# Weight chunks loaded in halves and split in quarters, with one TensorE wait per quarter

## What is computed

```python
h = jnp.pad(x @ w_in, ((0, 0), (PAD, 0), (0, 0)))
ya = window_gqa(qa, ka, va, sink) * jax.nn.silu(ga)        # A: banded attention, 4 heads
ob = diff_attention(qb, kb, vb, lam, valid)                # B: dense differential attention, 4 heads
y_f = hgrn2_chunked(qc, k_f, ic, logf_f)                   # C: gated linear recurrence, both directions
y = jnp.concatenate([ya, yb, yc], axis=-1)[:, PAD:]
return y @ w_out
...
h = layer_norm(ALPHA * h + y, ln_g[l], ln_b[l])
```

## Time and profile before

| | |
|---|---|
| median of 3 runs | 2032.49 us (2021.19 to 2033.53) |
| the profiled execution | 2035.93 us, of which the profile's span is 2034.6 us |
| mean granted clock of TensorE | 0.948 |
| PE busy | 1766.6 us (87%) |
| DVE busy | 1229.3 us (60%) |
| ACT busy | 885.6 us (44%) |
| POOL busy | 357.2 us (18%) |

### The profile page before, as it was taken

How to read it: one execution, slowest core, us unless ns; L and a number is a source line. 1 busy time by engine, 2 the same in 40 slices (tenths; PEclk the granted TensorE clock), 3 DMA queues, 4 the chain that set the end, 5 groups by cost and what they waited for, 6 DMA issues and landing times. The chain is left out here.

```text
span 2034.6 us, 37112 instructions
## 1 busy us (share of the span) xinstructions
PE 1766.6 (87%) x14474; PEld 1645.5 (81%) x14474; DVE 1229.3 (60%) x2793; ACT 885.6 (44%) x2700; POOL 357.2 (18%) x122
## 2 busy tenths in 40 slices
PE   3898999999879897968988989999998798987796
PEld 3888888899778786857988888889988687876696
DVE  7584683455457777874176746834554566767615
ACT  5334434245325564663053344352552254645603
POOL 5410211210120101010343102112102101101024
PEclk9899999999889999989999999999998899998998
DMA  6200100100100000032121001001001000002222
GB/s 240 62 22 11 53 22 26 49 25 12 51 21 7 27 9 26 14 126 91 42 100 58 22 12 53 22 28 47 27 13 46 22 9 27 29 6 101 79 87 83
DMA packets 97132, 91.85 MB, mean 45 GB/s; under 512 B 5120, under 2 KB 87280, under 8 KB 96960
## 3 DMA queue, kind: packets, MB, share of 16 engines
q1 hardware_dynamic: 96960, 89.49, 13.5%
HBM read 68.30 MB, written 21.17 MB: 44 GB/s over the span
## 5 line engine op out<-in xcount | busy, mean ns | idle before, releaser
L771 PE MATMUL psum<-w_hi,hT_hi 128*128 128x256 f32 x2400 | 710.6, 296 | 31.4 <-DVE rb L1661 15.0
L771 PE MATMUL psum<-w_hi,hT_lo 128*128 128x256 f32 x2400 | 688.4, 287 | 0.0
L771 PE MATMUL psum<-w_lo,hT_hi 128*128 128x256 f32 x2400 | 687.3, 286 | 0.0
L771 PEld LDWEIGHTS psum<-w_hi,hT_hi 128*128 128x128 f32 x2400 | 467.4, 195 | 42.5 <-issue 27.1
L771 PEld LDWEIGHTS psum<-w_hi,hT_lo 128*128 128x128 f32 x2400 | 467.1, 195 | 0.0
L771 PEld LDWEIGHTS psum<-w_lo,hT_hi 128*128 128x128 f32 x2400 | 466.3, 194 | 0.0
L739 POOL CAST w_hi<-w_raw 128x2048 fp32r<-128x2048 f32 (+1 forms) x42 | 81.5, 1942 | 1082.4 <-DMA w_raw<-in_w_in 1081.9
L1061 PE MATMUL psum<-vg_b,aT_b 128*128 128x128 f32 (+1 forms) x1224 | 159.4, 283 | 35.7 <-ACT aT_b L1361 35.7
L741 POOL TENSOR_TENSOR w_lo<-w_raw,w_hi 128x2048 fp32r<-128x2048 f32 (+1 forms) x42 | 189.1, 4503 | 3.4
L1800 DVE TENSOR_REDUCE row_max<-psum 128x1 f32<-128x1024 f32 x136 | 165.4, 1216 | 28.3 <-PE psum L912 28.2
L1061 PEld LDWEIGHTS psum<-vg_b,aT_b 128*128 128x128 f32 (+1 forms) x1224 | 146.0, 190 | 43.7 <-ACT aT_b L1361 41.0
(11 more groups left out here) (161 smaller groups left out, 2838.7 us busy)
## 6 DMA issues: line engine op xcount, KB each, us to landing
w_raw<-in_w_in SPq DMA_DIRECT2D x52, 512.0 KB, 4.9
h_dram<-hbuf SPq DMA_DIRECT2D x16, 512.0 KB, 2.6
w_raw<-in_w_out SPq DMA_DIRECT2D x8, 1024.0 KB, 5.1
hbuf<-h_dram SPq DMA_DIRECT2D x16, 512.0 KB, 5.8
qk_b<-y_dram SPq DMA_DIRECT2D x16, 512.0 KB, 3.3
y_dram<-y_stage SPq DMA_DIRECT2D x96, 64.0 KB, 1.6
w_raw<-in_w_in SPq DMA_DIRECT2D x6, 1024.0 KB, 5.4
hbuf<-in_x SPq DMA_DIRECT2D x8, 512.0 KB, 7.5
```

The costliest lines, as they stand in the source:

```text
L771: last = nc.tensor.matmul(out_ap, lhs[a](k), rhs[b](k), start=k == 0 and a + b == 0, stop=k == KT - 1 and b == 1)
```

## The change

Each transfer of a weight chunk becomes two, for the row blocks 0 to 3 and 4 to 7, each half with its own semaphore. `split_chunk` goes over the chunk in four pieces of two row blocks: wait for the half, multiply by the norm weights (for `w_out`, the last three pieces), cast, subtract, count `w_split` up by one. TensorE no longer waits for the whole chunk ahead of a unit; inside of the unit it waits at k = 0, 2, 4 and 6 for the piece that holds that k. No number that is computed changes, and nothing changes its place relative to other work.

```diff
 KT = DM // P
 CW = 256
+W_LOADS = 2
+W_PIECES = 4
+PIECE = KT // W_PIECES
...
-            for c0, n in CHUNKS[i][3]:
-                sp.dma_start(w_raw[:, i % 2, :, at:at + n], w[:, :, c0:c0 + n]).then_inc(w_loaded[i % 2], 16)
-                at += n
+            for j in range(W_LOADS):
+                ks = slice(j * KT // W_LOADS, (j + 1) * KT // W_LOADS)
+                at = 0
+                for c0, n in CHUNKS[i][3]:
+                    sp.dma_start(w_raw[:, i % 2, ks, at:at + n], w[:, ks, c0:c0 + n]).then_inc(w_loaded[i % 2][j], 16)
+                    at += n
...
-            pool.tensor_copy(w_hi[:, i % 2, :, 0:n], raw).then_inc(w_hi_done, 1)
-            pool.wait_ge(w_hi_done, i + 1)
-            pool.tensor_tensor(w_lo[:, i % 2, :, 0:n], raw,
-                               w_hi[:, i % 2, :, 0:n].bitcast(F32), ALU.subtract).then_inc(w_split, 1)
+            for j in range(W_PIECES):
+                ks = slice(j * PIECE, (j + 1) * PIECE)
+                raw, hi, lo = (w[:, i % 2, ks, 0:n] for w in (w_raw, w_hi, w_lo))
+                pool.wait_ge(w_loaded[i % 2][j * W_LOADS // W_PIECES], 16 * loads_before(i))
+                if g == "O" and j:
+
+                    pool.wait_ge(norm_w_in, 16)
+                    pool.tensor_tensor(raw, raw, view(norm_w, 0, P, l * 6 + (j - 1) * PIECE, [[1, PIECE], [0, n]]),
+                                       ALU.mult).then_inc(w_scaled, 1)
+                    pool.wait_ge(w_scaled, (W_PIECES - 1) * (l * (DM // CW) + name) + j)
+                pool.tensor_copy(hi, raw).then_inc(w_hi_done, 1)
+                pool.wait_ge(w_hi_done, W_PIECES * i + j + 1)
+                pool.tensor_tensor(lo, raw, hi.bitcast(F32), ALU.subtract).then_inc(w_split, 1)
...
-        def split_product(out_ap, lhs, rhs, ks=range(KT)):
+        def split_product(out_ap, lhs, rhs, ks, i):
             for k in ks:
+                if k % PIECE == 0:
+                    pe.wait_ge(w_split, W_PIECES * i + k // PIECE + 1)
                 for a, b in ((0, 0), (1, 0), (0, 1)):
...
             if half != 1:
-                pe.wait_ge(w_split, i + 1)
```

## The result

| | before | after |
|---|---|---|
| median of 4 runs | 2033.01 us (2021.19 to 2033.85) | **1969.7 us** (1965.45 to 1975.57) |
| ratio | | 0.9688, 95% interval 0.9655 to 0.972 |
| span of the profile | 2034.6 us | 1965.7 us |
| mean granted clock of TensorE | 0.948 | 0.960 |

The account below looks back on a forecast made before the run. The prediction took TensorE, busy for most of the span, as the bound, with roughly 100 us of stands at splits. Its terms summed to 25.8 us off 2035.93, 2010.1; it took 2009 us, range 1988 to 2036.

Parts of the forecast that it names:

- three signs of being wrong: 512-column pieces costing well over 1.34 us, first half not landing sooner, or stands in the levels staying as they are.
- Rival C: Holds matter to nothing; only TensorE's 9.4 us waits for the split come back: 2028 us; chance 0.38 together with A.
- rivals A and B: A: many short holds cost what long ones did, 2028 us (0.38 with C). B: GpSimd's extra time slows VectorE, 2063 (0.10).
- The tiny chain: Pass B, L1810 to L1814 each wait for a piece: 0 at first `w_out` chunk, -3.2 us at last `w_in` chunk.
- The rule of one operation for each boundary: One VectorE operation passes at each boundary between two GpSimd instructions; a held one waits out what is left of the instruction.
- the replay: Each site replayed with that turn-taking; at pass B's first `w_out` chunk the gain at L1666 is used up: 0 us.
- The levels: C's levels, 4 sites: step ready 2.4 us sooner, half of 1.8 us slow clock back; 4 x 3.1 = 12.4 us.
- Places left out: TensorE stands in or just behind about 25 of 42 splits, roughly 100 us; these places got no term.
- First gate chunks: First gate chunk of each layer: first unit overlaps the split, units behind still end with GpSimd; 0.7 each, 1.4 us.
- The start: First split lies between layer-norm additions; GpSimd 1.6 us longer, L1490 runs in the middle, TensorE's first stage hangs on it: -1.9 us.
- The halves: Weight loads cut in two cost nothing the rows show; first half there about 1.6 us sooner, GpSimd ends when it did before.
- Signs predicted for the profile: Casts 0.62, subtractions 1.34 us, no hold above 1.4, `k_sel` below 10, pass B's `qk_b` not shrinking, first matmul 2 us later.

Follow-up runs that it names:

- the first experiment: Changed kernel with only the wait on TensorE undone: it waits for all four pieces ahead of each unit, as before; 1977.15 us, ratio 0.9724.
- the ceiling: Changed kernel with nearly no split: GpSimd scales, casts and subtracts one column per row block, TensorE takes the high part twice; 1926.17 us, ratio 0.9477.
- the pass B kernel: Changed kernel with four pieces only for last keys and first two `w_out` chunks of each layer, others whole, loads in halves; 2010.52 us, ratio 0.9903.
- the partly cut kernels: Changed kernel, only some chunks in four pieces: pass B's three 2010.52 us, levels' two 2012.94, first `w_out` chunk (whole loads) 2015.45, all but those five 2001.37.
- the mixture: Changed kernel with whole loads, first chunk split whole, eight pieces for `w_out` and last `w_in` chunk, four elsewhere; 1958.55 us, ratio 0.9643.

## Why the prediction was wrong in size

The mechanism was right. VectorE held by GpSimd's long instructions is what the splits cost, shorter ones relieve it, and what TensorE waits for in its own units is the smaller part. None of the three signs of being wrong that the prediction named came up; it failed on the other side. Rival C (only the purpose stated works) falls with the first experiment, rivals A and B with the time. The upper limit given, 100 us of stands plus the clock, is where the ceiling was measured (107). What failed are terms of the sum, most of them too small. Gain by place, as predicted and as the lead of the changed kernel's units shows it (the leads sum to the 69 us between the two profiles, not to the 63 between the medians):

| place | predicted | measured |
|---|---|---|
| start of the kernel | -1.9 | -2.5 |
| first gate chunk of the layers | 1.4 | 5.4 |
| C's levels, 4 sites | 12.4 | 18.5 |
| keys of B's first head and of A | 8.2 | 10.6 |
| meta maxima | 3.8 | 3.8 |
| A's gates, first layer | 2.5 | 1.8 |
| pass B, last chunk of `w_in` | -3.2 | 1.8 |
| pass B, first chunk of `w_out` | 0 | 10.9 |
| pass B, second chunk of `w_out` | 2.6 | 6.5 |
| places with no term (other steps of the levels and of A, layer 1's start) | 0 | 11.8 |
| sum | 25.8 | 68.6 |

- **The tiny chain (failed step, 16 us).** "Five tiny operations, L1810 to L1814, now each wait for a piece" carried two terms, 0 and -3.2. In the first layer's pass at the first chunk of `w_out` the chain ran ahead of the split and met none of it, as it had before (L1814 at 779.19 us, the split from 779.23). VectorE and GpSimd after:

```profile
754.57 0.16 DVE L1821 TENSOR_TENSOR coef<-coef,neg_lam 128x1 f32<-128x1 f32 x1
```

```profile
755.39 1.15 POOL L746 CAST w_hi<-w_raw 128x512 fp32r<-128x512 f32 x1 [76.17 <-DMA w_raw<-in_w_out]
```

  In the other it was held for 2.1 us in three operations. The rule of one operation for each boundary was read off an operation of 1.3 us against another; two operations of 0.15 us pass at one boundary, the one with a single operand (L1811) needs no turn, or no instruction is under way. The prediction named passing in twos as not shown and put it at +5 us; the two places came out 16 us above their terms. Against those 2.1 us stand L1666 (3.89 us to 0.42, second layer) and L1825 (4.45 to 0.98, first layer), which the replay had let the chain eat up.
- **The levels (term mis-sized, 6 us).** The stand shrank by 2.8 us in the step shown, where 2.4 were predicted. The clock is what was halved: behind the stand of 1.2 us it stays at 1.00, and the unit behind it gained 1.5 us, nearly the whole 1.8 of the slow stretch. TensorE's busy time fell by 16 us over the kernel; the prediction had under 4 us of clock, all of it at the levels.
- **Places left out (failed step, 12 us).** Of about 25 stands with a split beside them the prediction priced 18 and the start. The others gave 3 us or less one by one, and the largest owes nothing to a split (luck). At 340 us before, TensorE stands 2.58 us for L1617 (L1624 after) in both profiles, with GpSimd idle. Windows of 1 us behind it, before and then after:

```profile
341.00:342.00 1.00, 1.00 (x6) 1.00 (x6) 0.00 (x0) 0.23 (x2) 0.00 (x0) 0.50 0.00 0
```

```profile
331.00:332.00 1.00, 1.00 (x10) 1.00 (x10) 0.00 (x0) 0.63 (x4) 0.00 (x0) 1.00 0.00 0
```

  Before, 0.50 lasted for nearly 7 us; after, the clock did not fall, and the lead grew from 9.8 to 12.8 us. In the other kernels the same stand is followed by 3 to 7 us at 0.50. So what the clock gives is not the splits' doing alone: TensorE's busy time is lower than before by 16 us with the change, by 20 with the wait undone, by 11 with four pieces and one load.
- **First gate chunks (4 us too small).** "The units behind it and VectorE's gates still end with GpSimd" was right in part: TensorE's first unit started 4.9 us earlier in both layers, it then stood for 0.9 and 1.4 us in the first and 1.0 and 1.2 in the second, and about half of the lead stayed.
- **The start (right sum, half of the cause).** It was put down to a longer split between the layer-norm additions. That split takes 9.6 us instead of 7.5, and what it costs the first unit is 1.1 of the 2.5 us. The other 1.4 are a later landing of `x`, which the prediction did not have and which comes up with whole loads too.
- **The halves** gave nothing beside pieces (1969.7 us with, 1969.24 without). That their first half is wanted early in two places only would explain it, but is argued. That they cost nothing in transfer fits the same two times.
- **Signs predicted for the profile.** Lengths of pieces, the longest hold (1.1 us), `k_sel` below 10, several short waits at the layers' starts, the first unit 2 us later (2.5): all seen. "The wait for `qk_b` in pass B does not shrink" was wrong.

What stays open is how the gain divides exactly between places, and why the halves alone give 7 us. Each edit also moves later splits against VectorE's work, as the first keys of B show, and the clock falls or not behind the same stand. At the first layer's first chunk of `w_out`, in four pieces in each, the lead grows by 6.8 us with the change but by 3.4 in the pass B kernel and 3.6 with the wait undone. The runs of the partly cut kernels scatter over 12 to 21 us, where the mixture scatters over 5. That the scatter comes from these causes was not tested.

## What to carry to other kernels

Where GpSimd and VectorE both work from SBUF, look for short VectorE operations that end exactly as a long GpSimd instruction does, and sum what they are over their own time; that sum, and a kernel with the GpSimd work cut to one column, give the ceiling before anything is rebuilt. Here, cutting the GpSimd work into instructions about as long as VectorE's own paid far more than its longer total cost, until the pieces' own cost caught up (between 4 and 8 pieces). Do not replay the turns over chains of tiny operations to find a loss: here that replay lost 16 us of gain. A stand of TensorE that gets short can give its clock back too, and that is part of the price of each stand, but compare several kernels before counting on it.

## What the runs showed of the hardware that was not expected

- An operation of 0.15 us of VectorE can pass behind a held one before the next instruction of GpSimd begins (L1820 above). The reciprocal, with a single operand, was not held in any of its five starts beside a running GpSimd instruction (L1818 above). The mean hold after the change is 0.6 us, half of a subtraction.
- A cast of 256 columns takes 0.40 us and a subtraction 0.73, of 512 columns 0.61 and 1.27: by the straight line the part that does not depend on the size is about 0.2 us. GpSimd with eight pieces:

```profile
138.66 0.40 POOL L763 CAST w_hi<-w_raw 128x256 fp32r<-128x256 f32 x1
139.14 0.73 POOL L765 TENSOR_TENSOR w_lo<-w_raw,w_hi 128x256 fp32r<-128x256 f32 x1
```

- At C0's level step, the stand of 4.0 us is followed by a granted clock of 0.50 and that of 1.2 us by 1.00. A stand of 2.58 us, the same in both profiles, was followed by 0.50 before and by 1.00 after.
- At the start, four weight issues in a row on SP took 6.5 us and two took 4.5; over all kernels it was 5.5 to 7.6 and 4.2 to 5.6.
